# Prompt scores of a hybrid decoder layer: from one fp32 product to three split fp32r products

## The reference

```
EVEN_SPLITS = (Q_LORA, KV_LORA, QK_ROPE, W_A, W_B, W_B, W_M, W_M)
...
def _mla_scores(q_lat, q_rope, lat, krope):
    s = jnp.einsum('bhqc,bkc->bhqk', q_lat, lat) + jnp.einsum('bhqr,bkr->bhqk', q_rope, krope)
    return s.astype(jnp.float32) * MLA_SCALE
...
        s = _mla_scores(ql, qr, latent, k_rope)
        qpos = i * ATTN_BLOCK + jnp.arange(ATTN_BLOCK)
        s = jnp.where(kpos[None, :] <= qpos[:, None], s, -jnp.inf)
        p = jax.nn.softmax(s, axis=-1).astype(latent.dtype)
        return jnp.einsum('bhqk,bkc->bhqc', p, latent)
```

## Time and profile before

| what | value |
|---|---|
| median of 3 runs | 1392.65 us (1390.35 to 1392.79) |
| the profiled execution | 1394.84 us, span 1393.2 us |
| granted TensorE clock, mean | 0.994 |
| busy share | PE 98%, DVE 59%, ACT 42%, POOL 8% |
| prompt scores (L1151) | 192 matmul records, 73.1 us |

### The profile page before, as it was taken

How to read it: one execution, slowest core, us unless ns; L and a number is a source line. 1 busy time by engine, 2 the same in 40 slices (tenths; PEclk the granted TensorE clock), 3 DMA queues, 4 the chain that set the end, 5 groups by cost and what they waited for, 6 DMA issues and landing times.

```text
span 1393.2 us, 24939 instructions
## 1 busy us (share of the span) xinstructions
PE 1364.7 (98%) x10020; PEld 1234.2 (89%) x10020; DVE 815.8 (59%) x1541; ACT 590.7 (42%) x1060; POOL 114.3 (8%) x213
## 2 busy tenths in 40 slices
PE   9999999999999999999999999999999999999996
PEld 9988999777767667689998898999999999999996
DVE  4486843275675676656885354324445649545687
ACT  4169622246656565533552333215553125212353
POOL 1000000000000305700002000010000010000000
PEclk9999999999999999999999999999999999999998
DMA  6211132210002147745665211134334131114562
GB/s 214 63 31 46 31 124 91 85 33 14 1 1 105 33 129 221 200 164 169 193 205 217 80 58 31 61 62 72 66 61 114 32 106 31 48 61 153 171 218 102
DMA packets 59300, 135.77 MB, mean 97 GB/s; under 512 B 9001, under 2 KB 37898, under 8 KB 58418
## 3 DMA queue, kind: packets, MB, share of 16 engines
q1 hardware_dynamic: 48882, 112.45, 25.4%
q0 software_dynamic: 10160, 21.56, 6.7%
q10 hardware_dynamic: 144, 0.18, 0.0%
HBM read 120.65 MB, written 13.50 MB: 96 GB/s over the span
## 4 chain that ended last, share of the span: by engine, by line
PE 84%; DVE 7%; issue 5%; ACT 2%; POOLq 1%; DMA 0%; POOL 0%; DVEq 0%; ACTq 0%
PE ps L578 15%; PE ps L580 14%; PE ps L579 14%; PE ps L710 5%; PE ps L712 5%; PE ps L711 5%; PE ps L1151 3%; PE ps L1188 2%; PE ps L1163 2%; PE ps L1323 2%; PE ps L591 1%; PE ps L3249 1%; DVE ln_sq L981 1%; PE ps L3244 1%; PE ps L1662 1%
## 5 line engine op out<-in xcount | busy, mean ns | idle before, releaser
L578 PE MATMUL ps<-x_hi,w_hi 128*128 128x352 f32 x1288 | 425.1, 330 | 0.0
L580 PE MATMUL ps<-x_hi,w_lo 128*128 128x352 f32 x1288 | 414.0, 321 | 0.0
L579 PE MATMUL ps<-x_lo,w_hi 128*128 128x352 f32 x1288 | 413.3, 321 | 0.0
L578 PEld LDWEIGHTS ps<-x_hi,w_hi 128*128 128x128 f32 x1288 | 241.7, 188 | 10.0 <-issue 9.5
L579 PEld LDWEIGHTS ps<-x_lo,w_hi 128*128 128x128 f32 x1288 | 242.7, 188 | 1.3 <-issue 1.0
L580 PEld LDWEIGHTS ps<-x_hi,w_lo 128*128 128x128 f32 x1288 | 241.7, 188 | 0.0
L520 ACT ACTIVATE w_hi<-w_raw 128x1024 fp32r<-128x1024 f32 (+1 forms) x105 | 121.3, 1155 | 235.6 <-PE ps L580 128.5
L526 DVE TENSOR_TENSOR w_lo<-w_raw,w_hi 128x1024 fp32r<-128x1024 f32 (+1 forms) x105 | 141.6, 1348 | 62.8 <-ACT w_hi L520 62.3
L710 PE MATMUL ps<-mx_hi,w_hi 128*128 128x352 f32 x480 | 155.6, 324 | 0.3 <-issue 0.2
L712 PE MATMUL ps<-mx_hi,w_lo 128*128 128x352 f32 x480 | 154.1, 321 | 0.0
L711 PE MATMUL ps<-mx_lo,w_hi 128*128 128x352 f32 x480 | 153.9, 321 | 0.0
(11 more groups left out here) (511 smaller groups left out, 1998.7 us busy)
## 6 DMA issues: line engine op xcount, KB each, us to landing
...
page<-in_cache_mla SPq DMA_DIRECT2D x128, 128.0 KB, 2.4
...
w_mem<-in_w_mem SPq DMA_DIRECT2D x2, 2048.0 KB, 10.7
```

Source lines behind the costliest of these rows:

```text
L578: pe.matmul(out, w_hi[:, (u + 1) % 2, kk], x_hi[:, k, chunk(c)], start=(k == 0), stop=False)
L579: pe.matmul(out, w_hi[:, (u + 1) % 2, kk], x_lo[:, k, chunk(c)], start=False, stop=False)
L580: mm = pe.matmul(out, w_lo[:, (u + 1) % 2, kk], x_hi[:, k, chunk(c)], start=False, stop=(k == KX - 1))
```

## The change

The scores become three fp32r products: high query by high keys, high query by low keys, low query by high keys. A unit of more than 512 keys is cut in two equal parts. ACT rounds each query block to q_hi (64 copies, three buffers), POOL subtracts (q_lo, 64). The copy of a k piece out of PSUM, by ACT, writes kT_hi directly; DVE's keys_lo subtracts that from the piece, which still stands in PSUM (two instructions of 64x512 for each k piece), and PE's next piece waits for it (kl_ready). POOL makes the low part of the keys' rope rows (rope_keys_lo, four times) and zeroes the empty rows (three memsets). The low keys lie on planes 4 to 7 of mx: the gates there go to memory (mxd, 2.16 MB, by POOL) before, and come back by SP behind w_uv after the attention. The first scores stand ahead of piece 11, the second half of the first pair's values; ACT copies that piece after the first exponentials. All rope loads of the sample stage stand on POOL behind the last q_lo. The weights w_if and a mask are loaded later.

```diff
-        kT = keep("kT", [P, 4, T])
+        kT_hi = keep("kT_hi", [P, 4, T], F32R)
+        kT_lo = place("kT_lo", [P, 4, T], M0 + 4 * ROWS, F32R)
...
-        MX_ORDER = [4, 9, 0, 1, 2, 3, 5, 6, 7, 8]
+        MX_ORDER = [9, 0, 1, 2, 3, 4, 5, 6, 7, 8]
...
-                s = scores_of(u)
-                for a in range(0, u.nk, 512):
-                    b = min(a + 512, u.nk)
-                    mm = pe.matmul(s[:, a:b], q_of(u), k_of(u, a, b), start=True, stop=True)
+                pe.wait_ge(prep_ev, PAIR_PIECE[u.h // 2] + 5)
+                pe.wait_ge(kl_ready, 2 + 2 * u.h if u.h < 2 else 4 * (u.h // 2) + 4)
+                pe.wait_ge(sg_sel, 4 + u.h if u.h < 2 else 7)
+                pe.wait_ge(ql_ready, HEAD_UNIT[n] + 1)
+                qh, ql = split_q_of(n)
+                w = u.nk // parts_of(u)
+                for a in range(parts_of(u)):
+                    s, ks = ps[:, u.bank + a, 0:w], (u, a * w, a * w + w)
+                    pe.matmul(s, qh, k_of(kT_hi, *ks), start=True, stop=False)
+                    pe.matmul(s, qh, k_of(kT_lo, *ks), start=False, stop=False)
+                    mm = pe.matmul(s, ql, k_of(kT_hi, *ks), start=False, stop=True)
...
             scores(0)
+            last_first_piece()
...
+            def query_hi(n):
...
+                act.activation(split_q_of(n)[0], q_of(UNITS[n]), ACT.Copy).then_inc(qh_ready, 1)
+
+            for k in (0, 1):
+                query_hi(k)
             exps(0)
+            last_first_piece()
             for n in range(len(UNITS)):
+                for k in ISSUE.get(n + 1, ()):
+                    query_hi(k)
...
                     sp.dma_start(w_uv[:, :, :, :], x["w_uv"]).then_inc(tbl_in, 16)
+                    sp.dma_start(mx[:, 4:8, :], mxd).then_inc(tbl_in, 16)
...
+            gp.wait_ge(lru_mul, 4)
+            gp.dma_start(mxd, mx[:, 4:8, :]).then_inc(spill, 16)
...
+            gp.memset(qT[32:64, 1:4:2, :], 0.0).then_inc(sg_sel, 1)
+            gp.memset(kT_hi[32:64, 1:4:2, :].bitcast(F32), 0.0).then_inc(sg_sel, 1)
+            gp.wait_ge(spill, 16)
+            gp.memset(kT_lo[32:64, 1:4:2, :].bitcast(F32), 0.0).then_inc(sg_sel, 1)
...
+            def rope_keys_lo(s):
+                r = 64 * (1 - s % 2)
+                gp.wait_ge(sg_sel, 3 + s)
+                gp.tensor_tensor(kT_lo[r:r + ROPE, s, :], z[0:ROPE, Z_KR, 0:T], kT_hi[0:ROPE, 1, :],
+                                 ALU.subtract).then_inc(sg_sel, 1)
+
+            def query_lo(n):
...
+                gp.tensor_tensor(lo, q_of(UNITS[n]), hi, ALU.subtract).then_inc(ql_ready, 1)
+            rope_keys_lo(0)
+            rope_keys_lo(1)
+            for n in HEAD_AT[0:3]:
+                query_lo(n)
...
+            for n in HEAD_AT[3:]:
+                query_lo(n)
             gp.wait_ge(tbl_in, 32)
...
-            v.mark(dve.memset(qT[32:64, 1:4:2, :], 0.0))
-            v.mark(dve.memset(kT[32:64, 1:4:2, :], 0.0))
...
+            def keys_lo(i, r):
+                what, p, j = piece_of(i)
+                rows, s, cols = slice(64 * r, 64 * r + 64), 2 * (p % 2) + r, slice(512 * j, 512 * j + 512)
+                dve.wait_ge(prep_ev, i + 1)
+                dve.tensor_tensor(kT_lo[rows, s, cols], ps[rows, piece_bank(i), 0:512], kT_hi[rows, s, cols],
+                                  ALU.subtract).then_inc(kl_ready, 1)
...
             def rope_at(n):
+                i = prep_at(n)
+                if i and piece_of(i)[0] == "k":
+                    for r in range(2):
+                        keys_lo(i, r)
...
                     pe.wait_ge(prep_ev, i)
+                    if piece_of(i - 1)[0] == "k":
+                        pe.wait_ge(kl_ready, 4 * piece_of(i - 1)[1] + 2 * piece_of(i - 1)[2] + 2)
```

More of the change, by code:

```diff
@@ L242, in build @@
         rec2 = keep("rec2", [P, 2, P])
-        rec4 = [[place("rec4_00", [P, P], S0 + 7296), place("rec4_01", [P, P], S0 + 7808)],
-                [place("rec4_10", [P, P], X0 - 512), place("rec4_11", [P, P], at["rec2"])]]
-        assert at["rq"] <= S0 + 7296 and at["rec4_01"] <= S0 + 2 * ROWS
+        rec4 = [place("rec4_0", [P, P], X0 - 512), place("rec4_1", [P, P], at["rec2"])]
+        q_at = (at["kT_lo"], Z0 + 14 * ROWS + 4096, Z0 + 14 * ROWS + 4608, S0 + 7296, S0 + 7808, at["masks"] - 512)
+        q_hi = [place(f"q_hi{n}", [P, P], q_at[2 * n], F32R) for n in range(3)]
+        q_lo = [place(f"q_lo{n}", [P, P], q_at[2 * n + 1], F32R) for n in range(3)]
+        assert at["rq"] <= S0 + 7296 and at["q_lo1"] <= S0 + 7808 and at["q_hi0"] <= M0 + 8 * ROWS
         wh = place("wh", [P, 2, 7 * P], W0)
@@ L1091, in q_of, with split_q_of, k_of @@
             return qT[rows_of_head(u.h), u.h % 4, u.q * P:u.q * P + P]
-        def k_of(u, a, b):
-            return kT[rows_of_head(u.h), u.h % 4, a:b]
+        def split_q_of(n):
+            b, rows = HEAD_UNIT[n] % 3, rows_of_head(UNITS[n].h)
+            return q_hi[b][rows, :], q_lo[b][rows, :]
+        def k_of(k, u, a, b):
+            return k[rows_of_head(u.h), u.h % 4, a:b]
         def part_done_at(n):
@@ L1108, in probs_of @@
             return probs[:, n % 2, 0:u.nk]
+        HEAD_AT = [n for n, u in enumerate(UNITS) if u.h is not None]
         FILLS, fill = {}, 0
@@ L3180, in rope_at @@
                     rope_sum(4 + n - 22)
+                    sample_rope(4 + n - 22)
                 elif n in (34, 35):
                     rope_sum(6 + n - 34)
+                    sample_rope(6 + n - 34)
                 else:
                     dve_between(dve, v, n)
+            rope_keys(1)
+            rope_keys(0)
+            v.settle()
+            dve.tensor_copy(col(1), eps[:, 0:1]).then_inc(kr_ready, 1)
             for step in range(3):
                 rope(0, step)
+            v.settle()
+            dve.wait_ge(spill, 16)
             for h in range(2):
                 rope_sum(h)
+                for i in (6, 7):
+                    keys_lo(i, h)
+            rope_keys(2)
+            rope_keys(3)
+            for h in range(2):
+                sample_rope(h)
+            v.settle()
+            dve.tensor_copy(col(1), eps[:, 0:1]).then_inc(kr_ready, 1)
             dve_attention(dve, v, rope_at)
@@ L3262, in _ @@
             pe.wait_ge(mem_ev, 5)
-            for i in range(N_FIRST):
+            for i in range(N_FIRST - 1):
                 if i == 4:
```

128 lines of the change are left out of this document (82 added, 46 removed).

## The result

The changed kernel takes 1416.72 us in the median of 4 runs (1415.97 to 1417.65) against 1392.72 for the kernel before: a ratio of 1.0168 (95% interval 1.0155 to 1.0182). It is 24.0 us slower, where 1390.5 was forecast, and outside the range of 1382.5 to 1397.5. The profiled execution took 1415.97, its span is 21.2 us longer than before. First the page: span and busy times.

What follows compares the result with a forecast made beforehand. PE was taken to bound the prompt attention, so shorter matmuls shorten the program. 8.7 - 6.0 + 0.5 - 0.5 - 0.6 = 2.1 us less than the profiled 1394.84, 1392.7, or 1390.5 beside the median; range 1382.5 to 1397.5.

Steps and rivals of the forecast that it cites:

- The start: Ahead of the first scores: DVE loses memsets and copies, POOL makes rope rows; middle taken, a gain of 0.5 us.
- the bound of -2.5: Ahead of the first scores: a loss of 2.5 us if POOL's key rows come 5 later.
- The third rival: POOL late ahead of the first scores: 1.5 to 4.5 us lost there, 1392.5 to 1395.5 in all; chance 0.12.
- its sign of 304: In the changed profile, first scores near 304 instead of near 300 if POOL is not in time.
- The pieces: Keys' pieces in the attention: waits for DVE's keys_lo shift PE's later work by 1.4, 2.5 and 2.1, 6.0 us.
- Its far bound, 8.6: The most the waits at the keys' pieces were to cost, called the holes' full sum: 8.6 us.
- the second rival: The clock falls in a new hole, about 3.4 us each: 1393.9 with one, 1397.3 with two; chance 0.19.
- The scores: Prompt attention: shorter score matmuls save 11.6 us, 10.9 without units 0 and 1, with 3.5 as the far end.
- Later on: From 500 to 531 an earlier PE waits longer in its holes; 0.5 us taken off (0 to 2).
- the rope loads: The sample stage's loads behind the last q_lo: last landing 1.4 earlier to 2.0 later; 0.6 us taken off.
- The spill: 2.16 MB go out beside w_mem's load: hidden, taken as 0, up to 5 us for a late first product.
- The copies q_hi and q_lo: 64 of each on ACT and POOL, issued a unit ahead and hidden behind PE's work: taken as 0.

Runs made afterwards that it cites:

- e2: The changed kernel with all four subtractions of the keys' rope rows done by DVE instead of POOL; 1405.46 us, ratio 1.0096.
- e12: The kernel before with two POOL subtractions of 32x1024 added beside DVE's first rotation; 1399.68 us, ratio 1.0045.
- e1: The changed kernel with POOL's third and fourth rope-row subtraction behind the tenth q_lo instead of the third; 1412.79 us, ratio 1.0130.
- e13: The kernel before with the two memsets of empty rows moved from DVE to POOL, behind the projections; 1389.86 us, ratio 0.9975.
- e3: The changed kernel with the nope rows' low part made zero and PE's next piece not waiting for DVE's keys_lo; 1402.73 us, ratio 1.0086.
- e6: e5 with one fp32 product per score in place of the three fp32r products; 1399.24 us, ratio 1.0039.
- e5: The changed kernel with the edits of e2 and e3 together; 1397.72 us, ratio 1.0031.
- e7: e2 with DVE's keys_lo ahead of into_mx in its loop, nothing left out; 1399.87 us, ratio 1.0053.
- e11: e7 with two rope-load rounds among late q_lo, DVE's last rope copies and sample rows in its loop, pair 2's rotation earlier and rope_sums later; 1396.05 us.
- e8: e2 with ACT also copying later keys pieces whole into kT_lo's place, where DVE subtracts, PE waiting for ACT alone; 1402.59 us, ratio 1.0061.

## Why the prediction was wrong, step by step

**The start (+0.5 in the sum; measured -5.7, beyond the bound of -2.5).** The first output is 6.46 late, 0.75 of which that execution brought from the projections. This step failed first. It priced POOL's subtractions by their own time (1.3 to 3.2, measured 2.34 and 3.24) and let them lie beside DVE's rotation, saying that nothing showed what the reads cost each other, and then took nothing for it. They cost DVE 4.0 us, in the middle of its way to the first query rows (e2, e12). It also overlooked what is queued on POOL: the second two subtractions stand ahead of the fourth q_lo and held unit 3 for 4.26 (e1). The third rival had POOL late, with at most 4.5 lost; the first scores at 303.17 are near its sign of 304, but POOL was in time and DVE was late. That the memsets are a gain was right: -4.7 at the first output in e13.

**The pieces (-6.0).** The holes were walked well: 2.0 and 2.2 for pair 2, measured 2.08 and 2.07; 2.1 for pair 1, measured 1.62; 0.9 and 2.1 for pair 3, measured 1.00 and 2.07. (Its far bound, 8.6, is not the sum of the five: that is 9.3, and 8.8 was measured.) What failed is the step that let the clock hold. It was the second rival, at 0.19 and with at most two falls; in the trace four stretches at the lower level follow the pieces' holes, and two more the start's holes of 3.68 and 4.26. By the clock in windows of 2 us the four cost 3.4, 1.7, 3.4 and 1.7 us of PE's time, where the rival took 3.4 for each. From first to last output the changed kernel lost 11.9 us, and e3, without the waits, gained 1.5; the holes sum to 8.8 there and the lost clock to 10.2, with the shorter scores against them.

**The scores (10.9 beside the start).** The direction was right and the size not: 6.2 in all, since each group of products costs about 0.1 us more than the cadence of a long run of triples says, and 128 columns come every 0.11 and not 0.066. Of the 6.2, 4.4 arrive (e6).

**Later on (-0.5) and the rope loads (-0.6).** Behind pair 3 the changed kernel gains 0.3 to the last output, so the 0.5 does not show. The wait for ropeT was 1.58 in the changed kernel, against 1.41. Behind the holes' removal it was 2.1 (e5), 0.7 more than before, with the lower clock behind it, so the loads are late by a little more than the 0.6. The spill cost nothing to see: the first w_mem product came at 247.6, in an execution that was already 0.75 later.

**The copies q_hi and q_lo (0).** Right but for the start: no other wait for q_lo is in the list of 303 to 620.

The 24.0, then, each run against the kernel before in its own round: e2 lies 13.4 above it, so 10.6 go with POOL's rope rows; e5 lies 4.9 above it, so another 8.5 go with the waits at the pieces; 4.9 are left. The parts are not independent: taken in the other order, the pieces' waits are 13.3 (e3 lies 10.7 above) and the rope rows 5.8; a hole brings the lower clock in one kernel and not in the other. What decides that stays open. With nothing left out, e7 lies 7.1 above and e11 2.4. Open, too, is a fall of the clock near 1125 us in the changed kernel (0.88 from 1124 to 1128, 0.69 from 1128 to 1132), in a stretch where PE waits for nothing. The change is not needed for it: it comes in e12 as well, the kernel before with two subtractions at the first rotation, and in e1, e2, e3, e8 and e11, but not in the other runs. In e12 (the clock is the last column but two):

```profile
1112.00:1116.00 4.00, 4.00 (x17) 4.00 (x17) 0.29 (x2) 0.28 (x1) 0.00 (x0) 0.57 0.00 0
```
